# Layer 1's sums of down weights: from VectorE to GpSimd, behind the spills of gate_up

## The reference

```
D_FF = -(-8 * D_MODEL // (3 * 256)) * 256        # 2816
def swiglu(h, w_gate_up, w_down):
    gate, up = jnp.split(h @ w_gate_up, 2, axis=-1)
    return (jax.nn.silu(gate) * up) @ w_down
...
    y = swiglu(h, w_gate_up[l], w_down[l])
    x = x + g2 * rms_norm(y, norm_gains[l, 3])
```

## Time and profile before

| | us |
|---|---|
| median of 3 runs | 2386.48 |
| lowest and highest | 2385.86, 2387.2 |
| the profiled execution | 2385.8 |
| its span | 2384.0 |
| TensorE busy in the span | 2332.9 (98%) |
| VectorE busy | 1616.9 (68%) |
| ScalarE busy | 979.8 (41%) |
| GpSimd busy | 287.4 (12%) |

### The profile page before, as it was taken

One profiled execution on the slowest core, in us unless ns is written; L12 is line 12 of the kernel. 1 busy time (PEld: TensorE's weight loads), 2 busy tenths in 40 slices (PEclk: granted clock), 3 DMA queues, 4 the chain that ended last, 5 costly groups with the idle time before them and its releaser, 6 DMA issues. The chain is left out here.

```text
span 2384.0 us, 30623 instructions
## 1 busy us (share of the span) xinstructions
PE 2332.9 (98%) x11394; PEld 1883.8 (79%) x11394; DVE 1616.9 (68%) x2718; ACT 979.8 (41%) x1870; POOL 287.4 (12%) x356
## 2 busy tenths in 40 slices
PE   7999999999999999999999999999999999999997
PEld 6788767788788888888778887777888888888886
DVE  6765677757877777576762556776687777655767
ACT  6312455544333333344763225555443333324454
POOL 0416400011000000220120110000200000003001
PEclk9999999999999999999999999999999999999999
DMA  7956511132554554663331111102324554227434
GB/s 288 328 202 201 163 27 27 48 120 79 163 174 150 188 183 141 185 208 97 125 125 45 37 36 45 28 27 80 115 71 168 185 197 174 80 71 234 150 103 153
DMA packets 210755, 311.29 MB, mean 131 GB/s; under 512 B 13063, under 2 KB 145080, under 8 KB 206640
## 3 DMA queue, kind: packets, MB, share of 16 engines
q1 hardware_dynamic: 182688, 205.50, 26.6%
q0 software_dynamic: 27920, 103.84, 13.3%
HBM read 243.48 MB, written 71.02 MB: 132 GB/s over the span
## 5 line engine op out<-in xcount | busy, mean ns | idle before, releaser
L3061 PE MATMUL ps<-hT,wsp 128*128 128x512 f32 x1440 | 333.5, 389 | 2.6 <-issue 2.6
L3061 PEld LDWEIGHTS ps<-hT,wsp 128*128 128x128 f32 x1440 | 270.0, 188 | 59.9 <-issue 4.0
L2591 PE MATMUL ps<-hT,wsp 128*128 128x512 f32 (+1 forms) x744 | 308.5, 415 | 0.0
L2593 PE MATMUL ps<-hT,wsp 128*128 128x512 f32 (+1 forms) x744 | 290.7, 391 | 0.0
L2592 PE MATMUL ps<-hT,wsp 128*128 128x512 f32 (+1 forms) x744 | 289.7, 389 | 0.0
L3100 PE MATMUL ps<-wsp,asp 128*128 128x512 f32 x1056 | 249.7, 392 | 0.2
L3100 PEld LDWEIGHTS ps<-wsp,asp 128*128 128x128 f32 x1056 | 198.1, 188 | 44.0 <-issue 1.0
L3061 PE MATMUL ps<-tsum,wasp 128*128 128x512 f32 x960 | 226.4, 391 | 0.0
L3061 PEld LDWEIGHTS ps<-tsum,wasp 128*128 128x128 f32 x960 | 180.2, 188 | 39.4 <-DVE wasp L2387 0.2
L2591 PEld LDWEIGHTS ps<-hT,wsp 128*128 128x128 f32 x744 | 140.9, 189 | 30.6 <-issue 7.8
L2593 PEld LDWEIGHTS ps<-hT,wsp 128*128 128x128 f32 x744 | 140.4, 189 | 30.7
(11 more groups left out here) (296 smaller groups left out, 4279.7 us busy)
## 6 DMA issues: line engine op xcount, KB each, us to landing
F<-in_w_mod SPq DMA_DIRECT2D x80, 512.0 KB, 5.4
raw<-in_w_in SPq DMA_DIRECT2D x48, 512.0 KB, 3.9
raw<-in_w_gate_up SPq DMA_DIRECT2D x48, 512.0 KB, 4.8
raw<-sums_d SPq DMA_DIRECT2D x88, 256.0 KB, 3.1
F<-in_w_gate_up SPq DMA_DIRECT2D x40, 512.0 KB, 5.6
acts_d<-F POOLq DMA_DIRECT2D x38, 512.0 KB, 6.6
F<-acts_d POOLq DMA_DIRECT2D x76, 256.0 KB, 4.4
raw<-in_w_down SPq DMA_DIRECT2D x66, 256.0 KB, 3.8
```

The lines of the kernel that those rows point to most:

```text
L2591: mm(o, a(0), b(0), start=start, stop=False)
L2593: return mm(o, a(1), b(0), start=False, stop=stop)
L3061: last = mm(bank(j, p), block_of(p, z)[:, k * P:k * P + P], times(p, zz, k), start=p < B_A22 and k == 0 and z == 0 and zz == 0, stop=k == ...
```

## The change

In layer 1, GpSimd forms the sums of block k right behind the issue of the spill of row j = k + 3, with the same four operations, in the same order, on the same buffers and with the same counts in s_bt. VectorE's `weight_sums` and `late_sums`, and the three calls of the latter, go. The operations of layer 0's `sums_make` move into the helper `sums_formed`, which both layers use, and the wait for the third count stands behind it. SP's loads and stores are as they were.

```diff
--- before.py
+++ after.py
@@ -958,18 +958,22 @@
                                    w_down.rearrange("l (a k p) n -> p l k a n", p=P, k=KH)[:, 0, k]
                                    ).then_inc(s_pl[SUMS_IN[k]], 16)
 
-                def sums_make(k):
-
-                    at = sums_made(0, k)
-                    b11, b12, b21, b22 = [sums_in(k)[:, HALF * i:HALF * i + HALF] for i in range(4)]
-                    pool.wait_ge(s_pl[SUMS_IN[k]], sums_moved(0, k))
+                def sums_formed(k, block, landed):
+
+                    at = sums_made(l, k)
+                    b11, b12, b21, b22 = [block[:, HALF * i:HALF * i + HALF] for i in range(4)]
+                    pool.wait_ge(landed, sums_moved(l, k))
                     nc.gpsimd.tensor_tensor(b22, b22, b12, ALU.subtract).then_inc(s_bt, 1)
                     nc.gpsimd.tensor_tensor(b12, b12, b11, ALU.subtract)
                     pool.wait_ge(s_bt, at + 1)
                     nc.gpsimd.tensor_tensor(b11, b11, b22, ALU.add).then_inc(s_bt, 1)
                     pool.wait_ge(s_bt, at + 2)
                     nc.gpsimd.tensor_tensor(b21, b21, b11, ALU.subtract).then_inc(s_bt, 1)
-                    pool.wait_ge(s_bt, at + 3)
+
+                def sums_make(k):
+
+                    sums_formed(k, sums_in(k), s_pl[SUMS_IN[k]])
+                    pool.wait_ge(s_bt, sums_made(l, k) + 3)
                     apart(pool)
                     pool.dma_start(sums_d[0, k], sums_in(k)).then_inc(s_pw[SUMS_IN[k]], 16)
 
@@ -1046,6 +1050,9 @@
                 for j in range(SPILLED):
                     pool.wait_ge(s_f2, l * JT + j + 1 + CREDIT)
                     pool.dma_start(acts_d[j], act_slot(j)).then_inc(s_as[j % KEPT_ACTS], 16)
+                    if l and 3 <= j < 3 + KH:
+                        k = j - 3
+                        sums_formed(k, sums_late(k % 2), s_bl[k % 2])
                 for j in range(SPILLED - KEPT_ACTS, SPILLED):
                     pool.wait_ge(s_as[j % KEPT_ACTS], spilled(l, j))
 
@@ -1931,22 +1938,6 @@
                     v.tensor_reduce(ast[:, A_NM + 2 * b + m:A_NM + 2 * b + m + 1],
                                     score_tile(b, m)[:, 0:n], AX.X, ALU.max, negate=True
                                     ).then_inc(s_mx, 1)
-
-                def weight_sums(k, part):
-
-                    at = sums_made(l, k)
-                    b11, b12, b21, b22 = [sums_late(k % 2)[:, HALF * i:HALF * i + HALF]
-                                          for i in range(4)]
-                    if part == 0:
-                        dve.wait_ge(s_bl[k % 2], sums_moved(l, k))
-                        v.tensor_tensor(b22, b22, b12, ALU.subtract).then_inc(s_bt, 1)
-                        v.tensor_tensor(b12, b12, b11, ALU.subtract)
-                    if part == 1:
-                        dve.wait_ge(s_bt, at + 1)
-                        v.tensor_tensor(b11, b11, b22, ALU.add).then_inc(s_bt, 1)
-                    if part == 2:
-                        dve.wait_ge(s_bt, at + 2)
-                        v.tensor_tensor(b21, b21, b11, ALU.subtract).then_inc(s_bt, 1)
 
                 def gla_tile(t):
 
@@ -2393,11 +2384,6 @@
                     dve.wait_ge(s_ss, (nth(l, j) - 1) * 4 + 3)
                     v.tensor_tensor(b, b, a, ALU.subtract).then_inc(s_ss, 1)
 
-                def late_sums(j, part):
-
-                    if l and 4 <= j < 4 + KH:
-                        weight_sums(j - 4, part)
-
                 def mod_chunks(qs):
 
                     for q in qs if l + 1 < L else ():
@@ -2453,7 +2439,6 @@
                     if more:
                         block_lo(j + 1, B_S2)
                     mod_chunks(share[0:1])
-                    late_sums(j, 0)
                     if j > PLAIN:
                         third_sum(j)
                     if more:
@@ -2467,13 +2452,11 @@
                     if more:
                         block_lo(j + 1, B_S1)
                     mod_chunks(share[1:2])
-                    late_sums(j, 1)
                     dve.wait_ge(s_sp, seven(l, j, B_A22))
                     v.tensor_tensor(tile[:, 0:HALF], bank(j, B_A22), u2, ALU.add).then_inc(s_u, 1)
                     if more:
                         block_lo(j + 1, B_A22)
                     mod_chunks(share[2:3])
-                    late_sums(j, 2)
                     if not more:
                         down_lo(0)
                         down_lo(1)
```

## The result

| | before | changed |
|---|---|---|
| median, us | 2386.64 (4 runs) | 2420.81 (4 runs, 2418.24 to 2421.24) |
| ratio, 95% interval | | 1.0142 (1.013 to 1.0154) |
| profiled execution, its span | 2385.8, 2384.0 | 2418.24, 2416.4 |

The account below looks back on a forecast made before the run. TensorE alone was taken to bound the kernel. Relief 0, added work 0 and 11 x 0 of stall gave 0 against the profiled 2385.8 us, so 2386.5 for the median; the likeliest case's range was 2385 to 2391, overall to 2406.

Parts of the forecast that it names:

- What bounds the kernel: Layer 1's stretch with the moved sums: TensorE alone, busy 210.00 of 210 us, nearest to waiting at B_A22 behind third_sum.
- The idle slack of 1.83 + 1.20 us: Between third_sum and B_A22, 1.83 us plus 1.20 us of VectorE's relief: 3.0 us of delay before TensorE waits.
- VectorE's relief: Four subtractions fewer per block in 11 blocks, 26.4 us of VectorE's time, counted as 0.0 us on the path.
- The queues: Later spill on POOL, store and weight loads on SP, block's load already landed: room enough, zero cost for all.
- The step that failed: At the sums' start behind the spill, GpSimd asks while VectorE is inside L2379, so the engines take turns; stall 0.
- the sign that was named: In the changed profile, VectorE's L2387 of wa lasting 3 us or more would show the forecast wrong.
- The row of 83.40: Layer 0's VectorE operation of 4.89 us, 3.61 longer, standing through three GpSimd operations that ran with nothing between them.
- the rival with a chance of 0.30: VectorE stands through three GpSimd operations, third_sum makes TensorE late at B_A22; 2404 to 2406 us, chance 0.30.
- The price of a turn: Each VectorE operation with two SBUF tensors ahead of third_sum has one GpSimd operation ahead: 1.03 us longer, 1.25 at most.
- The stall of 0 in that branch: In turns, third_sum ends 0.1 to 0.6 us before B_A22 needs it; no TensorE stall, 2386.5 us, chance 0.50.
- The price of three in a row: At B_A22, TensorE stalls 1.6 us in each of 11 rows, 17.6 us; upper end 1.8 us, 19.8 in all.
- The rival that was drawn from the Trainium skill: GpSimd's cores start the next instruction at once, ports never free between operations: three in a row, 2404.1 us, chance 0.30.

Follow-up runs that it names:

- e1_none: Changed kernel with GpSimd's four operations left out, layer 1's sums formed by neither engine; 2386.14 us, ratio 0.9997.
- e6: Changed kernel with the sums ahead of the spill's issue on POOL; 2394.42 us, ratio 1.0033.
- e5: Changed kernel with a wait for VectorE's second block sum between the spill and the sums; 2385.95 us, ratio 0.9997.
- e9: Changed kernel with the sums started while VectorE is idle ahead of the low half of B_S4, the row's spill following them; 2392.06 us, ratio 1.0025.
- e13: e9 with two GpSimd memsets of 512 and 576 columns ahead of the first operation; 2404.22 us, ratio 1.0076.
- e12: e5 with the wait for VectorE's second block sum ahead of the spill, so the sums stand right behind the DMA issue; 2386.11 us, ratio 1.0001.
- e2: Changed kernel with the four operations started only when third_sum of the next row is done; 2387.0 us, ratio 0.9999.
- e10: e9 with the spill of the row before issued right ahead of the sums, in the same VectorE idle time; 2406.08 us, ratio 1.0088.
- e14: Changed kernel with one GpSimd memset of 64 columns between the spill's issue and the four operations; 2421.64 us, ratio 1.0148.
- e4: Changed kernel with four memsets of the same 128x512 tiles in place of the four operations; 2386.65 us, ratio 1.0001.

## Why the prediction was wrong

- **What bounds the kernel** held: TensorE alone, and B_A22 behind third_sum the point nearest to a wait (11 of 11 stalls stand there). The idle slack of 1.83 + 1.20 us held: 5.12 us of hold-up (4.04 on L2370, 1.08 on L2378) less some 1.3 us of VectorE's idle time made third_sum 3.85 us late, of which 1.83 us were hidden.
- **VectorE's relief costs and brings nothing**: held (e1_none, 0.9997).
- **The queues** (store on SP, spill on POOL, the block's load): held. The store goes out 6.2 us behind the spill.
- **The step that failed** is "In the row, GpSimd asks at 1895.64 while VectorE is inside L2379 (1895.33), as it asked at 74.10 inside a VectorE operation; there turns were taken." I dated GpSimd's claim by the start of its first operation and took VectorE's head start of 0.31 us for possession. What the runs show in its place: L2379 (L2370 after), which asks during the DMA issue, 0.38 us ahead of the first operation, is held for 4.04 us, through three operations, in 11 of 11 rows. GpSimd's first operation had not "to wait for VectorE" as the prediction had it: it lasts 1.31 us. So the sign that was named (L2387 of wa at 3 us or more) isn't the one that came, it lasts 1.77 us; rows longer by over 0.4 us came.
- **Why the two rows of layer 0 differ.** The row of 83.40 had shown the hold, and I had named it as the rival with a chance of 0.30; the DMA issue directly ahead, which it shares with the changed kernel, was written down for it and weighed too little. At 74.10 a DMA issue (of the bias, at 73.31) stood ahead as well. What was different there is that VectorE asked 0.39 us behind the first operation's start: in the six executions in which the same place is asked for within 0.06 us, it is held too.
- **The price of a turn** was right: 1.03 to 1.25 us were taken, 1.01 to 1.10 measured. Whether turns at this very place would have cost nothing no run shows. In e6, where the first operation starts 0.81 us earlier in the row and turns are taken, the second block sum is held as well, and the cost is 7.9 us (ratio 1.0033); in e5, where it starts 0.40 us later, turns cost nothing. The stall of 0 in that branch is neither confirmed nor refuted.
- **The price of three in a row** was 17.6 us, bound 19.8, and 34.2 came (32.4 in the profiled execution). A row's stall was put at 1.6 us and is 2.16, since the hold began one operation earlier, so that one more operation of 0.60 us was still to come behind it. Starting again costs 0.12 us (36 matmuls in 8.44 for 8.32 us). That makes 25.2 us; another 6.4 us are the clock, for which the sum had no term at all. No row of before bore on it, since TensorE never stands in this stretch; but where a stall is forecast, the clock behind it belongs among the unknown costs.
- **Two rules of the Trainium skill**: by the order of issue ("SBUF — State Buffer", section "Who interferes with whom") VectorE, with its earlier start, should have finished L2370 first; the 4.73 us speak against this reading. The rival that was drawn from the Trainium skill, "GPSIMD Engine Reference", section "2.1 Instruction dispatch", with the added assumption that the ports never come free between two operations, gave the right pattern; but by it VectorE should be held through three with no DMA ahead as well, and in e9 and e13 it isn't. So it isn't the cause by itself.

**What stays open** is the mechanism by which a DMA issue lets the three operations keep VectorE out. Shown is only when it happens: reading operations without a wait between them, a DMA issue right ahead (one memset may stand between), and a VectorE request between 0.46 us before and 0.13 us behind the first one's start, held every time (39 rows of four kernels, and 22 blocks of layer 0). At 0.28 to 0.43 us behind VectorE got in (10 of 10, layer 0). At 0.76 us and more behind it got in in 7 rows and was held in 4 (e12); what parts these isn't known, so the time of asking alone is not the rule.

No version beat the kernel before. TensorE has no idle time in the stretch, so the best that moving the sums can do is to cost nothing (e1, e2, e5 and e12, all within 0.2%). In e12 that hangs on 0.2 us in 4 of the rows.

## What to carry to other kernels

Before work moves to GpSimd beside a VectorE that "has room", find VectorE's operation with the tightest consumer, list those ahead of it that have two tensors in SBUF, and put GpSimd's work behind it: the same 44 operations (four in each of 11 rows) cost 34 us right behind a DMA issue and nothing after third_sum. Don't let a run of GpSimd operations stand directly behind a DMA issue of its own without waits in between. A waiting time of TensorE of 2 us in steady work costs more than its length, since the clock may fall behind it.

## What the runs showed of the hardware

- GpSimd and VectorE take turns by whole operations, 1.01 to 1.10 us more for each VectorE operation of 128x512 with two SBUF tensors that meets a whole one of GpSimd's or nearly, also when GpSimd's operations stand back to back and the first met no one (e9, e13). VectorE's operations of 128x512 with one tensor in PSUM are at 0.68 or 0.69 us in this stretch in all runs.
- Right behind a DMA issue of GpSimd they don't when VectorE asks close to the first operation's start: 4.04, 3.59 and 4.14 us of hold in the changed kernel, e10 and e14, each time ending 0.56 us behind the third operation. At 0.76 us behind that start it is 4 rows held (by 2.91 us) to 7 in turns (e12).
- A GpSimd memset of 128x512 takes 0.52 to 0.55 us and holds none of VectorE's operations up (0.68 and 0.69 us, e4).
- The granted clock fell to 0.50 for some 3 us behind idle times of TensorE of 1.95 to 2.01 us in 5 of 17 rows, and in 7 of 11 each behind 2.03 to 2.09 and 2.31 us, not behind 1.78 us or less (66 rows); each fall costs 1.6 us.
